# Part of a depthwise convolution on GpSimd instead of TensorE

## What is computed

```python
def conformer_conv(a, gate, dw_kernel, dw_bias, ln_g, ln_b):
    u = a * jax.nn.sigmoid(gate)
    pad = CONV_WIDTH // 2                       # CONV_WIDTH = 31
    y = lax.conv_general_dilated(
        u, dw_kernel[:, None, :], window_strides=(1,), padding=[(pad, pad)],
        dimension_numbers=("NWC", "WIO", "NWC"), feature_group_count=u.shape[-1])
    y = y + dw_bias
    y = layer_norm(y, ln_g, ln_b)
    return jax.nn.silu(y)
```

## Time and profile before

| | us |
|---|---|
| median of 3 runs | 1049.14 |
| lowest and highest | 1047.73, 1053.33 |
| the profiled execution | 1050.84 |
| its span in the trace | 1049.0 |

### The profile page before, as it was taken

How to read it: one execution, slowest core, us unless ns; L and a number is a source line. 1 busy time by engine, 2 the same in 40 slices (tenths; PEclk the granted TensorE clock), 3 DMA queues, 4 the chain that set the end, 5 groups by cost and what they waited for, 6 DMA issues and landing times.

```text
span 1049.0 us, 16345 instructions
## 1 busy us (share of the span) xinstructions
PE 1030.5 (98%) x6205; PEld 895.4 (85%) x6205; DVE 707.7 (67%) x1073; ACT 535.9 (51%) x687; POOL 69.6 (7%) x80
## 2 busy tenths in 40 slices
PE   8989999999999999999999999999999999999997
PEld 7865788888888899998888888888999988888886
DVE  6876776666667686768666656667776677655655
ACT  6545575444457534455645444475344646444443
POOL 1000000000000309000000000011170000000000
PEclk9989999999999999999999999999999999999999
DMA  9975345555556653248465563665632674565521
GB/s 295 218 223 176 104 139 199 201 170 195 180 185 186 201 176 121 80 164 294 147 223 179 189 211 105 226 202 163 198 101 81 221 241 165 196 206 195 170 90 41
DMA packets 130653, 185.13 MB, mean 176 GB/s; under 512 B 4361, under 2 KB 106399, under 8 KB 130591
## 3 DMA queue, kind: packets, MB, share of 16 engines
q1 hardware_dynamic: 130503, 184.25, 54.4%
q10 hardware_dynamic: 88, 0.04, 0.0%
HBM read 180.91 MB, written 1.56 MB: 174 GB/s over the span
## 4 chain that ended last, share of the span: by engine, by line
PE 93%; DVE 2%; ACT 1%; DMA 1%; SPq 1%; issue 1%; DVEq 0%; ACTq 0%
PE wide L561 19%; PE wide L568 10%; PE acc L524 9%; PE acc L525 9%; PE acc L526 9%; PE wide L524 7%; PE wide L525 7%; PE wide L526 7%; PE wide L544 3%; PE wide L537 3%; PE wide L538 3%; SPq L438 1%; PE acc L704 1%; PE acc L738 1%; DMA big<-cu 1%; PE acc L725 1%
## 5 line engine op out<-in xcount | busy, mean ns | idle before, releaser
L1294 DVE TENSOR_TENSOR wlo<-raw,whi 128x2048 fp32r<-128x2048 f32 (+1 forms) x178 | 387.1, 2181 | 156.7 <-ACT whi L980 155.6
L980 ACT ACTIVATE whi<-raw 128x2048 fp32r<-128x2048 f32 (+1 forms) x178 | 322.1, 1819 | 105.5 <-PE wide L526 43.9
L561 PE MATMUL wide<-uhl,whi 128*128 128x512 f32 x864 | 207.3, 391 | 0.0
L561 PEld LDWEIGHTS wide<-uhl,whi 128*128 128x128 f32 x864 | 160.7, 188 | 33.7 <-DVE uhl L1319 1.2
L524 PE MATMUL acc<-whi,mhi 128*128 128x512 f32 x376 | 147.8, 393 | 0.3 <-DVE mlo L1372 0.3
L524 PE MATMUL wide<-uhl,whi 128*128 128x256 f32 x512 | 147.0, 287 | 1.0 <-DVE wlo L1379 0.9
L525 PE MATMUL acc<-wlo,mhi 128*128 128x512 f32 x376 | 146.9, 391 | 0.0
L526 PE MATMUL acc<-whi,mlo 128*128 128x512 f32 x376 | 146.5, 390 | 0.0
L525 PE MATMUL wide<-uhl,whi 128*128 128x256 f32 x512 | 144.9, 283 | 0.0
L526 PE MATMUL wide<-uhl,wlo 128*128 128x256 f32 x512 | 144.9, 283 | 0.0
L568 PEld LDWEIGHTS wide<-uhl,wlo 128*128 128x128 f32 x864 | 110.8, 191 | 4.2
(11 more groups left out here) (248 smaller groups left out, 1218.6 us busy)
## 6 DMA issues: line engine op xcount, KB each, us to landing
raw<-in_w_in SPq DMA_DIRECT2D x49, 1024.0 KB, 5.3
raw<-in_w_mlp_up SPq DMA_DIRECT2D x32, 1024.0 KB, 5.5
raw<-in_w_mlp_down SPq DMA_DIRECT2D x32, 1024.0 KB, 4.9
raw<-in_w_gate SPq DMA_DIRECT2D x11, 1024.0 KB, 5.3
raw<-in_w_up SPq DMA_DIRECT2D x11, 1024.0 KB, 5.4
raw<-in_w_down SPq DMA_DIRECT2D x11, 1024.0 KB, 5.5
raw<-in_w_mix_out SPq DMA_DIRECT2D x8, 1024.0 KB, 6.6
raw<-in_w_out SPq DMA_DIRECT2D x4, 1024.0 KB, 10.5
```

The costliest lines, as they stand in the source:

```text
L561: pe.matmul(col[2 * n + c][:], whi_v(u)[:, f, c * P:c * P + P], uhl[:, f, :], start=f == 0, stop=False)
L980: act.activation(whi[:, u.buf, 0:size], raw[:, u.slot, 0:size], ACT.Copy).then_inc(w_hi, 1)
L1294: dve.tensor_tensor(wlo[:, u.buf, 0:size], raw[:, u.slot, 0:size], whi[:, u.buf, 0:size].bitcast(F32), ALU.subtract).then_inc(w_lo, 1)
```

## The change

`TAP_START` gives for each channel group the first tap group that `convolve` runs: 4, 4, 3 and 2, where it was 4, 4, 0 and 0. The three first tap groups of c = 2 (12 taps) and the two first of c = 3 (8 taps) are done by GpSimd: for each tap a product of the shifted `cu` and the tap's column, broadcast, into `y` (the first) or into `rnb`, and a sum into y. It starts when the taps are in SBUF and glu is 2. A new semaphore, conv_pool, tells that c is done; `conv_evac(2)` and `conv_evac(3)` wait for it and become one instruction that adds bank, bias and y.

```diff
+TAP_START = (DVE_SETS, DVE_SETS, 3, 2)
...
+        conv_pool = sem("conv_pool")
...
             def convolve(c):
-                first = DVE_SETS if c < 2 else 0
+                first = TAP_START[c]
...
-                dve.tensor_scalar(y[:, c, :], CONV_BANK[c][:, 0:T], gcol[:, G_DWB + c:G_DWB + c + 1], None, ALU.add)\
-                    .then_inc(conv_sb, 1)
+                dve.wait_ge(conv_pool, c - 1)
+                dve.scalar_tensor_tensor(y[:, c, :], CONV_BANK[c][:, 0:T], gcol[:, G_DWB + c:G_DWB + c + 1], y[:, c, :],
+                                         ALU.add, ALU.add).then_inc(conv_sb, 1)
...
+            pool.wait_ge(kx_sb, 2)
+            pool.wait_ge(glu, 2)
+            for c in (2, 3):
+                for w in range(TAP_START[c] * SHIFTS):
+                    tap = kcol[:, w * KA + c:w * KA + c + 1]
+                    out = y[:, c, :] if w == 0 else rnb[:]
+                    link(pool.tensor_tensor(out, cu[:, c, w:w + T], tap.broadcast_to([P, T]), ALU.mult))
+                    if 0 < w < TAP_START[c] * SHIFTS - 1:
+                        link(pool.tensor_tensor(y[:, c, :], y[:, c, :], out, ALU.add))
+                pool.tensor_tensor(y[:, c, :], y[:, c, :], out, ALU.add).then_inc(conv_pool, 1)
+                pool.wait_ge(conv_pool, c - 1)
```

## The result

The changed kernel takes 1055.47 us (median of 8, 1054.44 to 1057.48), the kernel before beside it 1050.08 us (median of 8, 1047.73 to 1053.33): a ratio of 1.0049 [1.0033, 1.0065], some 5 us slower. The forecast was 1053 us with a range of 1047.2 to 1057.0 us.

The account below looks back on a forecast made before the run. TensorE, busy 98%, was taken as the bound, with VectorE as close to the path. +6.3 - 2.2 = +4.1 us on the profiled 1050.84 us gave 1054.9 us, against the lower median 1053 us; range 1047.2 to 1057.0 us.

Parts of the forecast that it names:

- The gain: TensorE's convolutions of channel groups 2 and 3 lose five tap groups: 2.2 us less, between 1.9 and 2.3.
- The turns: VectorE's 21 taps alternate with GpSimd's operations: 0.84 us a turn, 9.2 us more in all; chance 0.50.
- The first rival: VectorE's taps aren't interrupted; later splits and stationary products wait instead: +0.2 us, 1049.3 us; chance 0.25.
- The cover: VectorE's idle 5.20 us hides most of its delay; ktok's sum of squares starts 4.4 us late.
- The clock: TensorE's clock falls to 1.2 GHz after new idle time ahead of ktok's turning: about 2.6 us lost, hidden.
- the third rival: TensorE idles 3 us more before convolution 2, which then runs at 1.2 GHz: 1058.9 us; chance 0.17 including GpSimd finishing late.
- The evacuations, GpSimd's end: Evacuations of groups 2 and 3 read y and wait for GpSimd: costed at nothing, GpSimd done by 90 us.
- The size: Whole kernel: 6.3 us of lateness less 2.2 us gained, +4.1 us.
- the lateness of the second scores: TensorE's second pair of scores waits for VectorE's second row maximum: 3.9 + 2.4 = 6.3 us late.

Follow-up runs that it names:

- e1: Changed kernel without GpSimd's 38 operations and the evacuations' wait and addition, 20 taps left out of y: 1048.64 us beside 1050.19 us before, ratio 0.9982.
- e5: Changed kernel with only 8 taps on GpSimd, one tap group from each of channel groups 2 and 3: 1050.81 us beside 1049.81 us before.
- e9: Changed kernel with only 12 taps on GpSimd, two tap groups of channel group 2, one of 3: 1051.42 us beside 1049.81 us before.
- e2: Changed kernel keeping GpSimd's work and the wait, but TensorE does all tap groups and evacuations overwrite y: 1058.16 us beside 1050.19 us before.
- f1: Kernel before plus 12 matmuls of zeros ahead of convolution 0, where TensorE waits for the shifted copies: median 1047.9 us, ratio 0.9993.
- e3: Changed kernel with GpSimd's operations replaced by 76 memsets into y, 20 taps left out, evacuations overwriting y but still waiting: ratio 0.9988 to before.
- e7: Changed kernel with only channel group 3's 8 taps on GpSimd, started after the second row maximum: 1050.61 us beside 1049.81 us before.
- f2: Changed kernel plus 12 matmuls of zeros ahead of convolution 0: 1054.43 us beside 1050.63 us before, ratio 1.0047.
- f3: Changed kernel with 12 taps on GpSimd and each of its operations cut into two of 128 tokens: 1050.25 us beside 1050.63 us before.
- e8: Changed kernel with each GpSimd operation cut into two of 128 tokens, nothing left out: 1050.49 us beside 1049.81 us before.
- e4: Changed kernel with GpSimd starting only after the first two adding evacuations: 1053.71 us beside 1050.19 us before.
- f4: Changed kernel with 12 taps on GpSimd, halved operations and 12 matmuls of zeros ahead of convolution 0: 1050.49 us beside 1050.63 us before.

## Why the prediction was right, and which term was too small

**The gain.** 2.2 us forecast; B fell by 2.16 us after, 1.98 us in e1, the clock falling once in all three. Right.

**The turns.** 0.84 us a tap forecast, 0.82 measured in the runs of eight. The 21 taps take 16.98 us (2.87 + 6.55 + 4.21 + 3.35) instead of 8.7 us, so 8.3 us more, not 9.2: the first four, beside GpSimd's first operations, take only 0.72 us each. The splits cost 0.4 instead of 0.3 us each. The adding evacuations end at 73.87 us, not 74.6. The first rival is out.

**The cover.** The idle 5.20 us hid as much as was said, and e5 and e9 show the edge of it: 8 taps fit, 12 don't quite. ktok's turning came at 76.94 us (forecast 77.8), the wait ahead of it was 2.66 us (3.8). VectorE had scaled ktok 3.1 us late (3.9 forecast), and behind that lost 2.7 us more (2.4 forecast): 1.9 us in the four stationary products (two took 2.23 instead of 1.29 us), 0.4 us in the split ahead of them, 0.4 us in a scaling of a maximum, and nothing in the last split, for which GpSimd waited instead. The two misses partly cancel. The second scores came at 88.89 us, 5.86 us late; forecast 6.3.

**The clock.** It fell as forecast, to 0.55 and 0.59 in 78 to 82 us, but cost less. TensorE itself was through with unit 9 at 88.89 − 1.90 = 86.99 us, 3.96 us late, of which 2.95 us were the wait: 1.0 us for the clock, not 2.6. The kernel before waits 0.59 us for ScalarE ahead of its first scores (77.46 us), the changed one doesn't: with that the fall took 1.6 us, as it did in e2's convolution 2. The step had read it off the first convolution, where it cost 2.6 us in this trace (f1 has the second scores 24.55 us after that convolution's start, before 27.11 us). Since VectorE was later anyway, it didn't matter; but it left TensorE 1.90 us idle, where the forecast had nothing to spare. That the clock then held at the second scores is partly luck: behind 1.88 us in e2 it fell, and the third rival, which asked for 3 us of idle time, may have been priced too low.

**The evacuations, GpSimd's end.** No wait for GpSimd: it ended at 87.8 us (by 90 forecast), the evacuation of group 2 took 0.48 us.

**The size.** Trace against trace it is 1052.6 − 1049.0 = 3.6 us for the forecast 4.1. The medians are 5.4 us apart, since the profiled execution of the changed kernel was the fastest of its eight (1.0 us under the median) and that of the kernel before 0.8 us over its own. The mis-sized term is the lateness of the second scores, for a reason that lies in the reckoning: it was counted against one execution of the kernel before, and there TensorE had itself been late, with copies that came late and a clock that fell. Where nothing holds VectorE, A is 37.55 (before), 37.80 (e1), 35.43 (e3) and 34.35 us (e7), 36.3 us on average. Where GpSimd does, it is 43.64, 43.65 and 43.67 us (after, e2, f2): VectorE's own chain sets it, and an early TensorE gains nothing. So the change costs 43.65 − 36.3 = 7.4 us in A and gives 2.2 us back in B, 5.2 us in all, near the 5.1 to 5.4 us measured. The same reckoning gives 43.65 − 36.3 = 7.4 us for e2 (8.0 us measured). Where TensorE's own part of A varies, one trace doesn't do: f3's would give 40.01 − 36.3 − 1.3 = 2.4 us slower, and −0.4 us was measured. That the mean of A in unprofiled executions is 36.3 us is inferred from four traces; f1, which should show what the variation is worth, was not clear of no change. The other 0.9 us between 1053 and 1055.47 us is the kernel before itself, whose median was 1049.14 us over three runs and 1050.08 us over eight.

## What to carry to other kernels

GpSimd is not free help beside a VectorE that combines two SBUF tensors: ask of each helper operation whether it reads SBUF (the memsets, which didn't, cost nothing here), and charge every such VectorE instruction beside it what is left of one helper operation, until VectorE's next idle time. Short helper operations lower that price. And a slack read from one execution is that execution's: where a DMA's arrival or a clock that falls sets the path before, look at several traces before you count how late is late.

## What the runs showed of the hardware

- **Readers hold a tap, writers don't.** 0.41 us a tap beside memsets that fill GpSimd's time (e3), 0.58 us beside operations of 128 elements (e8), 0.82 us beside those of 256.
- **It isn't only instructions with two tensors.** The scaling of probabilities (one SBUF tensor, a scalar per partition) took up to 1.53 instead of 0.62 us beside GpSimd in e4 and e7, and the scaling of a 128x2 maximum 0.56 instead of 0.17 us in the changed kernel, while the reduction kept its 1.21 us. The same page of the Trainium skill (same section) says that a tensor_scalar can enter a mode that contends and a reduction never does; the rows agree.
- **Idle lengths and the clock.** Behind waits of 2.66 us (after), 3.50 us (e2) and 3.81 us (before) TensorE ran at the lower level; behind 1.90 us it ran at full speed in the changed kernel, but behind 1.88 us in e2 at 0.50. The same wait of 2.03 us was followed by the lower level in twelve of the fourteen traces and by full speed in two, and e7 kept 1.00 behind 3.52 us of waiting for the copies. What tells these apart, the runs don't settle.
- **What a fall costs.** Behind the wait of 2.03 us the products and the mean took 1.61 + 3.11, 1.91 + 2.81, 1.08 + 3.61 or 1.79 + 2.93 us (before, after, e1, e5): the clock falls earlier or later, but the sum is 4.7 us each time, against 3.07 us where it stays. At the first convolution the price isn't fixed: from its start to ktok's turning, less the wait for VectorE, it is 15.5 to 15.7 us in the five traces in which the granted clock stays at 1.00 (e4, e7, f1, f2, f4), and 16.9 (e1) to 18.5 us (e9) in the others. The matmuls ran at 0.5 for some 3.2 us in e1, 5.2 us in the kernel before and 5.6 us in e9, and took 1.4, 2.6 and 3.0 us longer: about half of that time.
